# Attention in a diffusion block: heads taken in pairs, scores issued two pairs ahead, part of the score eviction moved to ScalarE

## The reference, cut to what matters

```python
scale = NA_HEAD_DIM ** -0.5                      # 64 ** -0.5 = 0.125
# latent ("local") queries: 256 latent keys with a bias, and 256 context keys without one
s_loc = einsum(q_r, k_b) * scale + bias          # bias masks all but the neighbourhood
s_ctx = einsum(q_r, k_ctx) * scale
p = softmax(concatenate([s_loc, s_ctx], -1))
o = p_loc @ v_b + p_ctx @ v_ctx
# context queries, in the first layer only (the last layer drops them): 256 context keys
s = einsum('bqhd,bkhd->bhqk', q, k) * scale
o = softmax(s) @ v
```

## Time and profile before

| what | value |
|---|---|
| median of 3 runs | 3099.96 us (3099.4 to 3101.96) |
| the profiled execution | 3101.26 us, its span 3099.5 us |
| mean granted TensorE clock | 0.954 of 2.4 GHz |
| `Mix` in layer 0 | about 563.6 to 645.8 us |
| `Mix` in layer 1 | about 1549.4 to 1603.1 us |

### The profile page before, as it was taken

How to read it: one execution, slowest core, us unless ns; L and a number is a source line. 1 busy time by engine, 2 the same in 40 slices (tenths; PEclk the granted TensorE clock), 3 DMA queues, 4 the chain that set the end, 5 groups by cost and what they waited for, 6 DMA issues and landing times. The chain is left out here.

```text
span 3099.5 us, 46116 instructions
## 1 busy us (share of the span) xinstructions
PE 2884.9 (93%) x15682; PEld 2422.1 (78%) x15682; DVE 2186.3 (71%) x4187; ACT 1235.7 (40%) x2282; POOL 369.4 (12%) x413
## 2 busy tenths in 40 slices
PE   7999999999999999999999997596479999999997
PEld 4888878567888778887859996376368999999997
DVE  2999994559898975657466664365997777777775
ACT  2323243443232332224354453153125555444554
POOL 0111116001111100100400000000473000000000
PEclk9999999999999999999999998798559999999999
DMA  5555443133545444544415556023003655666563
GB/s 233 177 176 203 170 142 102 34 109 136 197 173 194 178 162 143 185 142 148 130 49 170 180 175 216 0 69 109 1 0 96 188 185 187 186 186 188 184 189 115
DMA packets 107703, 449.94 MB, mean 145 GB/s; under 512 B 11952, under 2 KB 12592, under 8 KB 94256
## 3 DMA queue, kind: packets, MB, share of 16 engines
q1 hardware_dynamic: 93744, 347.46, 35.2%
q0 software_dynamic: 13824, 100.67, 8.6%
HBM read 447.04 MB, written 1.05 MB: 145 GB/s over the span
## 5 line engine op out<-in xcount | busy, mean ns | idle before, releaser
L178 DVE TENSOR_TENSOR weight_lo<-weight_ring,weight_hi 128x512 fp32r<-128x512 f32 x1272 | 945.5, 749 | 530.8 <-ACT weight_hi L171 515.8
L171 ACT ACTIVATE weight_hi<-weight_ring 128x512 fp32r<-128x512 f32 x1272 | 800.8, 632 | 1164.4 <-PE bank L257 1163.5
L255 PE MATMUL bank<-operand_hi,weight_hi 128*128 128x256 f32 (+1 forms) x3168 | 1039.4, 328 | 24.0 <-DVE operand_lo L592 13.0
L256 PE MATMUL bank<-operand_lo,weight_hi 128*128 128x256 f32 (+1 forms) x3168 | 1034.7, 327 | 0.0
L257 PE MATMUL bank<-operand_hi,weight_lo 128*128 128x256 f32 (+1 forms) x3168 | 1034.5, 327 | 0.0
L255 PEld LDWEIGHTS bank<-operand_hi,weight_hi 128*128 128x128 f32 x3168 | 603.7, 191 | 91.8 <-issue 21.4
L256 PEld LDWEIGHTS bank<-operand_lo,weight_hi 128*128 128x128 f32 x3168 | 603.9, 191 | 54.6
L257 PEld LDWEIGHTS bank<-operand_hi,weight_lo 128*128 128x128 f32 x3168 | 603.8, 191 | 50.8
L850 DVE SCALAR_TENSOR_TENSOR extension_ffn<-extension_ffn,silu_c 128x512 f32<-128x512 f32 x532 | 388.7, 780 | 1.7
L255 PE MATMUL bank<-hidden_hi_ffn,weight_hi 128*128 128x512 f32 (+1 forms) x704 | 256.6, 364 | 4.0 <-DVE arena L1095 4.0
L256 PE MATMUL bank<-hidden_lo_ffn,weight_hi 128*128 128x512 f32 (+1 forms) x704 | 255.3, 363 | 0.0
(11 more groups left out here) (260 smaller groups left out, 2740.1 us busy)
## 6 DMA issues: line engine op xcount, KB each, us to landing
weight_ring<-in_ffn SPq DMA_DIRECT2D x272, 512.0 KB, 3.6
weight_ring<-in_experts SPq DMA_DIRECT2D x256, 512.0 KB, 3.6
extension_ffn<-in_w_mods POOLq DMA_DIRECT2D x96, 1024.0 KB, 7.5
weight_ring<-in_w_mix SPq DMA_DIRECT2D x56, 512.0 KB, 3.6
weight_ring<-in_w_second SPq DMA_DIRECT2D x52, 512.0 KB, 4.0
extension_mixer<-in_rel_bias SPq DMA_DIRECT2D x2, 1536.0 KB, 6.8
arena<-in_x SPq DMA_DIRECT2D x1, 2048.0 KB, 9.4
arena<-in_cmp_k SPq DMA_DIRECT2D x1, 2048.0 KB, 11.8
```

Of the source, the lines that this page charges most:

```text
L171: nc.scalar.activation(self.hi[:, g % 2, h], self.ring[:, g % NS, h], ACT.Copy).then_inc(self.rounded, 1)
L178: self.nc.vector.tensor_tensor(self.lo[:, g % 2, h], self.ring[:, g % NS, h], self.hi[:, g % 2, h].bitcast(F32), ALU.subtract).then_inc(se ...
L255: nc.tensor.matmul(out, a_hi, b_hi, start=start and n == 0, stop=False)
L256: nc.tensor.matmul(out, a_hi, b_lo, start=False, stop=False)
```

## The change

The score scale is moved: `MixIn` multiplies the query chunks (8 to 11) by 0.125 in the copy out of PSUM that it makes anyway. The items are taken in pairs of heads: item 2n is the even head and item 2n + 1 the odd head of the same query half. `scores(n)` now makes both products of a pair, with four banks (0, 1, 6, 7) instead of two, and pair `w/2 + 2` is issued behind `transposes(w)` at even w. `values` now covers four items (two heads, two query halves): its products alternate between the heads, into rows 0 to 63 and 64 to 127 of one bank, and are issued as four parts, one behind each of four `transposes`. There is one `move` per four items, of 128 rows. For a local item ScalarE gets a new copy, `carry(w)`, of the 256 columns without bias, and VectorE's work is one addition of the bias (L1405 in the changed kernel) and the reduction. For a context item nothing is copied: VectorE reduces the bank itself, and ScalarE's exponential reads the bank.

```diff
@@ MixIn.scalar
-            nc.scalar.activation(self.u[:, n, 0:self.width[n]], chip.bank[n % 4][:, 0:self.width[n]], ACT.Copy)\
+            nc.scalar.activation(self.u[:, n, 0:self.width[n]], chip.bank[n % 4][:, 0:self.width[n]], ACT.Copy,
+                                 scale=DH ** -0.5 if CH_Q <= n < CH_K else 1.0)\
@@ Mix.__init__
-        self.items = [(g, h, qt) for g in range(ng) for h in range(NA_H) for qt in range(2)]
+        self.items = [(g, 2 * hp + j, qt) for g in range(ng) for hp in range(NA_H // 2) for qt in range(2) for j in range(2)]
+    def score_bank(self, w):
+        return (0, 1, 6, 7)[w % 4]
@@ Mix.tensor
-        for w in range(3):
-            scores(w)
+        scores(0)
         pe.wait_ge(evicted.sem, evicted.at(20))
+        scores(1)
         for w in range(len(items)):
-            if w + 3 < len(items):
-                scores(w + 3)
             transposes(w)
-            if w >= 2 and w % 2 == 0:
-                values(w // 2 - 1)
-        values(len(items) // 2 - 1)
+            if w % 2 == 0 and w // 2 + 2 < len(items) // 2:
+                scores(w // 2 + 2)
+            if w >= 4:
+                values(w // 4 - 1, w % 4)
+        for part in range(4):
+            values(len(items) // 4 - 1, part)
@@ Mix.scalar
+            if g and w >= 4:
+                act.wait_ge(self.turned.sem, self.turned.at(w - 3))
+        def carry(w):
+            if w >= self.local:
+                return
+            act.wait_ge(self.scored.sem, self.scored.at(w + 1))
+            if w >= 4:
+                act.wait_ge(self.turned.sem, self.turned.at(w - 3))
+            nc.scalar.activation(sc[:, w % 4, S:T2], chip.bank[self.score_bank(w)][:, S:T2], ACT.Copy)\
+                .then_inc(self.carried.sem, 1)
+        for w in range(3):
+            carry(w)
         exps(0)
         exps(1)
         for w in range(len(items)):
             if w + 2 < len(items):
                 exps(w + 2)
             copies(w)
+            if w + 3 < len(items):
+                carry(w + 3)
@@ Mix.vector, scale(w)
             if g == 0:
+                dve.wait_ge(self.carried.sem, self.carried.at(w + 1))
-                nc.vector.scalar_tensor_tensor(s[:, 0:S], bank[:, 0:S], 0.125, bias[:, h, r0:r0 + S], ALU.mult, ALU.add)
-                nc.vector.tensor_scalar(s[:, S:T2], bank[:, S:T2], 0.125, None, ALU.mult)\
+                nc.vector.tensor_tensor(s[:, 0:S], bank[:, 0:S], bias[:, h, r0:r0 + S], ALU.add)\
                     .then_inc(self.scores_read.sem, 1)
-            else:
-                nc.vector.tensor_scalar(s[:, 0:n], bank[:, 0:n], 0.125, None, ALU.mult)\
-                    .then_inc(self.scores_read.sem, 1)
```

More of the change, by code:

```diff
@@ L1204, in __init__ @@
         self.a, self.c = chip.part(A_POOL, ng, self.wide), chip.part(A_POOL + 544, ng, self.wide)
-        self.items = [(g, h, qt) for g in range(ng) for h in range(NA_H) for qt in range(2)]
+        self.items = [(g, 2 * hp + j, qt) for g in range(ng) for hp in range(NA_H // 2) for qt in range(2) for j in range(2)]
         n = len(self.items)
-        self.scored, self.scores_read, self.maxed, self.exped, self.probs, self.turned, self.copied = (
-            s.take(n) for s in (chip.scored, chip.scores_read, chip.maxed, chip.exped, chip.probs, chip.turned, chip.copied))
-        self.product, self.moved, self.mixed = chip.product.take(n // 2 + 1), chip.moved.take(n // 2), chip.mixed.take(1)
+        self.local = sum(g == 0 for g, _, _ in self.items)
+        self.scores_read, self.carried = chip.scores_read.take(self.local), chip.carried.take(self.local)
+        self.scored, self.maxed, self.exped, self.probs, self.turned, self.copied = (
+            s.take(n) for s in (chip.scored, chip.maxed, chip.exped, chip.probs, chip.turned, chip.copied))
+        self.product, self.moved, self.mixed = chip.product.take(n // 4 + 1), chip.moved.take(n // 4), chip.mixed.take(1)
         self.y_there = chip.y_there.take(2)
@@ L1259, in tensor, with scores @@
         evicted = self.mix_in.evicted
[L1261 to L1269, removed]
+        def scores(n):
+            if n >= 2 and 2 * n - 3 < self.local:
+                pe.wait_ge(self.scores_read.sem, self.scores_read.at(2 * n - 2))
+                pe.wait_ge(self.carried.sem, self.carried.at(2 * n - 2))
+            elif n >= 2:
+                pe.wait_ge(self.exped.sem, self.exped.at(2 * n - 2))
+            for w in (2 * n, 2 * n + 1):
+                g, h, qt = items[w]
+                lo, hi = keys(g)
+                po, q0 = 64 * (h % 2), g * S + qt * P
+                nc.tensor.matmul(chip.bank[self.score_bank(w)][:, 0:hi - lo], u[po:po + 64, CH_Q + h // 2, q0:q0 + P],
+                                 u[po:po + 64, CH_K + h // 2, lo:hi], start=True, stop=True)\
+                    .then_inc(self.scored.sem, 1)
         def transposes(w):
@@ L1345, in scalar @@
             copies(w)
-            if w >= 3 and w % 2 == 1:
-                move(w // 2 - 1)
-        move(len(items) // 2 - 1)
-        act.wait_ge(self.product.sem, self.product.at(len(items) // 2 + 1))
+            if w + 3 < len(items):
+                carry(w + 3)
+            if w >= 8 and w % 4 == 1:
+                move(w // 4 - 2)
+        move(len(items) // 4 - 2)
+        move(len(items) // 4 - 1)
+        act.wait_ge(self.product.sem, self.product.at(len(items) // 4 + 1))
         for b in range(2):
```

57 lines of the change are left out of this document (32 added, 25 removed).

## The result

| | median of 5 (us) | lowest to highest | profiled execution | its span | mean TensorE clock |
|---|---|---|---|---|---|
| before | 3099.96 | 3099.4 to 3103.9 | 3101.26 | 3099.5 | 0.954 |
| changed | 3116.39 | 3114.52 to 3118.68 | 3116.78 | 3115.0 | 0.945 |

The changed kernel takes 1.005 times as long (95% interval 1.0035 to 1.0064), 16.4 us more. The forecast was 3132 in a range of 3100 to 3144.

A forecast was written before the change was run, and what follows sets the result against it. TensorE was taken to set the pace of `Mix`, with a small wait for VectorE, and a ring afterwards. Layer 0 +16.8 and layer 1 +17.1 made +33.9, less 2: +32, 3132 us by the median, range 3100 to 3144.

The forecast's parts named there:

- The ring: Local items of `Mix`: a closed chain of waits across engines, one item long, sets the pace at 3.4 or 3.85 us.
- six links: Local items: addition to reduction 0.45, `normalise` 0.80, transposes 0.54, `copies` 0.69 (1.15 at 1.2 GHz), ScalarE's next 0.50, new copy 0.39.
- The 13 steps: Local items, first to 14th transposes in each layer: 13 x 3.85 = 50.1 us, +10.7 in layer 0, +11.0 in layer 1.
- the one on the clock: TensorE in `Mix`: the clock falls at the first wait and stays at 1.2 GHz through the local items.
- both pooling products: The product ending each layer of `Mix`, run at 1.2 GHz: +1.8 us in layer 0, +1.0 in layer 1.
- layer 1's end: Layer 1, 14th transposes to pooling product: 10.65 us against 6.4 before, +4.2.
- the 2 that had been taken off: Context items: 2 us subtracted from the sum because the clock may rise there.
- The first rival: Local items: the ring holds but at 2.4 GHz, +5.9 us, 3106 in all; chance 0.28.
- the second rival: TensorE in `Mix`: the heads don't run together; about 3120, up to 3170 if the clock stays down; chance 0.10.
- The third rival's last part: Local items: no closed ring, throughput sets a step of some 2.0 us, about 3066; chance 0.02 of the rival's 0.10.
- The heads run together: TensorE in `Mix`: products on different halves overlap, so a local pair's 3.9 us of scores and values take 2.0.
- Costed at nothing: `MixIn` scale, wider SBUF buffer, reduction or exponential reading PSUM, and 128-row `move`: all priced at no time.

The follow-up runs named there:

- carry_first: Changed kernel with `carry(w + 3)` moved ahead of `exps(w + 2)` and `copies(w)` on ScalarE: 3071.95 us, ratio 0.9902 to the kernel before.
- carry_twice_spare: Changed kernel with a second ScalarE copy of the same 128x256, into a spare buffer, just ahead of each `carry`: 3124.31 us, ratio 1.0074 to the kernel before.
- heads_apart: vector_copies with the two heads' scores, and their `values`, no longer issued side by side on TensorE but with other products between: 3091.57 us.
- kept_warm_2: Changed kernel with 8 and 3 added useless TensorE products by turns ahead of local items' transposes, from the third item on: 3108.84 us.
- vector_copies: Changed kernel with the 256-column copy made by VectorE behind its addition instead of ScalarE's `carry`: 3064.69 us, ratio 0.9882 to the kernel before.
- copies_shared: vector_copies with ScalarE's `carry`, placed first, for odd local items and VectorE's copy for even ones: 3064.82 us, ratio 0.9885 to the kernel before.

## Why the prediction was right in its sign and twice too large in its size

**The ring: right.** It was forecast as one chain, one item long, with six links in sequence. All six stand in the timeline above. Moving `carry` away from behind `copies` took 44 us off (carry_first), putting 0.26 us into it added 0.34 and 0.27 a step on average (53.61 - 49.17 and 53.72 - 50.26, over 13; the clock's ups and downs differ between the two kernels) (carry_twice_spare). The 13 steps cost +9.9 and +11.2 where +10.7 and +11.0 were forecast, so close because two errors cancelled (next point).

**One link was sized too small.** "the new copy of 128x256 ... 0.39" counted the instruction's duration; from its start to the addition's start it was 0.51, with 0.13 between the end of the one and the start of the other. The allowance of 0.03 for "the extra semaphore waits" did not cover that: the steps were 3.49 and 3.95 us, not 3.4 and 3.85. At 26 steps this is 2.6 us. It hid an error of the other sign, the clock's within the steps: at 3.95 throughout the 26 steps would take 102.7 us, at 3.49 throughout 90.7, and they took 99.4, 3.3 less than the first.

**The step that failed is the one on the clock**: "So I take it that the clock stays down through the local items." It went up and down inside them. More important, the same sentence carried the context items ("At 1.2: 16 x 1.7 + 4.5") and both pooling products. From the 14th transposes on, layer 0 was forecast at +3.4 and gave -8.5: 11.9 of the 15.9 us between forecast and result. The rest is the pooling products (1.8 and 1.0), layer 1's end (2.6) and the steps (0.6), less the 2 that had been taken off.

The price at the other level was sound: from the 16th transposes to the pooling product it was put at 20.0 us at 2.4 GHz, and 19.5 were measured; at 1.2 it was 31.7. At the end of layer 1, the two local items took 4.2 us (1608.03 to 1612.23) where 5.0 were forecast, and the last four parts of `values`, forecast at 4.0, took 2.05 to the pooling product at 1616.08, by this row of the timeline (weight loads):

```profile
1614.03 1.67 PEld L1307 LDWEIGHTS bank<-extension_mixer 128*64 128x64 f32 x16 [0.46 <-ACT extension_mixer L1362]
```

The granted clock was 0.99 from 1614.3 to 1616.0 and 0.50 before it, so most of the 2.6 is the clock again.

The prediction had worked out the price of the context items at both levels (-8.6 against +3.1) and said that "the clock may rise in them", and took off 2 of 11.7. What I leant on was the stretch of 83 us at 94% busy and 1.2 GHz; it is in another part of the kernel, and the nearer evidence, that in this very place the clock had risen before, was put second. For the clock in the context items alone I should have given both levels at least the same weight. That the result lies in the range is owed to the range's width: it covers the case at 2.4 GHz (3106) and the case at 1.2 (3120 to 3143), and 3116 belongs to neither.

The Trainium skill ("TensorE: Matmul & The Clock Gate", section "What's actually happening") says that activity releases the throttled state. In the changed kernel the trace agrees: the clock rose at about 624.5, after TensorE had been busy 8.65 of 10.5 us, and had fallen at about 614, after 5.33 of 10. In heads_apart it does not: the clock stayed at 0.50 while TensorE was busy 27.69 of 27.70 us. Why it stays down there, and why it alternates in the ring, is open.

**The first rival** (ring at 2.4 GHz, 3106) is kept_warm_2: 3108.8, or 3106 and the 0.09 us a step that both levels lacked (2.3 us). The real kernel lies between the two cases, which were priced as the only ones. In the second rival the prediction also took for granted that a TensorE without gaps makes the clock rise; layer 0 of heads_apart shows 27.7 us without a gap at 1.2 GHz.

**The third rival's last part** (throughput alone, 3066) did not happen in the changed kernel, but it is near what the kernels without a ring of one item took: 3064.7 (vector_copies) and 3072.0 (carry_first).

**The heads run together: right**, and now measured (1.13 us for four records that take 1.12 for two when apart).

**Page rule on eviction.** The Trainium skill, "TensorEngine Tiling (Array Packing)", section "PSUM Bottleneck", advises both ScalarE and VectorE for the eviction of PSUM. For the scores, VectorE alone gives 3064.7 here, both with the copy in the order of the change 3116.4, both with the copy first 3072.0, and the two by turns 3064.8. The place of the copy in ScalarE's order decides, not the sharing.

**Costed at nothing: right** as far as rows show. Groups by form of the changed kernel, 563 to 644 us, for the context items (count, busy us, mean ns, idle):

```profile
L1342 ACT ACTIVATE extension_mixer<-bank,nmax 128x256 f32<-128x256 f32 x16 | 7.6, 476 | 0.0
...
L1408 DVE TENSOR_REDUCE nmax<-bank 128x1 f32<-128x256 f32 x16 | 6.7, 421 | 8.0 <-PE bank L1281 8.0
```

The exponential that reads PSUM took 476 ns where it took 509 from SBUF; the read of its row sum behind it took 210 ns on average, against 189 over all items before, so the gain is small. The reduction took 421 from PSUM and 420 from SBUF before. The scale in `MixIn` has no run of its own; the span outside `Mix` changed by -0.5 us.

## What to carry to other kernels

Before moving a small instruction from a full engine to an emptier one, write down what stands ahead of it in the new queue and follow each wait back: if the loop comes back to the same instruction one item later, every link is paid in full, however idle the engines are. Here the copy, 0.4 us a local item, made the difference between 36 us gained (left on VectorE, vector_copies), 29 gained (on ScalarE, placed first) and 16 lost (on ScalarE, behind `copies`). Where TensorE's load falls, price every stretch at both clock levels and weigh them apart, since one stretch's level says little of the next. And try the plain variant as well: vector_copies, with no new wait at all, was the fastest, with copies_shared, which ties with it: 36 us under the kernel before.

## What the runs showed of the hardware

- In a regular ring of equal items the clock alternated between 1.2 and 2.4 GHz, in both layers of the changed kernel (means 0.71 and 0.60). It was at 2.4 GHz from 604 to 614 us, with TensorE busy 5.33 us of 10; then it fell, and was at 1.2 in the next 10.5 us, with 8.65 busy, before it rose again. With a few short products in the gaps (kept_warm_2) it was 1.00 from 580 to 616 us and from 1566 to 1602.
- A TensorE without gaps can stay at 1.2 GHz: heads_apart, 27.69 us busy of 27.70 at a clock of 0.50. Its layer 1 runs the same code on local items, and had 0.86 over 33 us; its executions spread over 14 us.
- Products on separate halves of the rows, and of the columns, overlap in full at 512 and 256 columns: 1.13 us for four score records of two heads and 1.12 for two of one head; 0.65 for four records of `values` of two heads and 0.65 for two of one head (heads_apart).
- ScalarE's exponential of 128x256 took less from PSUM than from SBUF, 476 ns against 509, and the read of its row sum 210 against 189.
- An added product of 128x128 in float32 is two records in the trace (16 records for 8 products in kept_warm_2), 0.11 us apart from start to start, where four transposes of that size are four.
